# Prompt attention: queries and keys in high and low parts, near scores as three fp32r products of 128 rows, and the third pair's load issued sooner

## The reference, cut to what matters

```python
GROUPS = ((128, 1), (512, 4), (2048, 16))        # (window, dilation)
scale = HEAD_DIM ** -0.5
# for each group, on strided sub-sequences in blocks of 128 queries:
s = jnp.einsum('brnqhc,brnkhc->brnhqk', qg, kb) * scale
s = jnp.where(mask[None], s, NEG_INF)
m = jnp.max(s, axis=-1, keepdims=True)
p = jnp.exp(s - m)
den = jnp.sum(p, axis=-1)
o = jnp.einsum('brnhqk,brnkhc->brnqhc', p, vb) / den[..., None]
# the three groups are combined per head, weighted by den * exp(m - m_top)
```

## Time and profile before

| | us |
|---|---|
| median of 3 runs | 1893.93 (1889.38 to 1894.47) |
| the profiled execution | 1889.74 |
| its span, first to last instruction | 1888.0 |
| mean granted TensorE clock | 0.999 of full |

### The profile page before, as it was taken

One profiled execution on the slowest core, in us unless ns is written; L12 is line 12 of the kernel. 1 busy time (PEld: TensorE's weight loads), 2 busy tenths in 40 slices (PEclk: granted clock), 3 DMA queues, 4 the chain that ended last, 5 costly groups with the idle time before them and its releaser, 6 DMA issues.

```text
span 1888.0 us, 35926 instructions
## 1 busy us (share of the span) xinstructions
PE 1859.1 (98%) x15206; PEld 1772.4 (94%) x15206; DVE 1209.6 (64%) x1507; ACT 710.3 (38%) x948; POOL 666.3 (35%) x339
## 2 busy tenths in 40 slices
PE   8999999999999999999999999999999999999998
PEld 8999999989889898679999999899999999999998
DVE  8899653255444645674456746884555575878988
ACT  6311221244434445664200034424444445433333
POOL 0122111211111113443466641136777761432514
PEclk9999999999999999999999999999999999999999
DMA  5422433766676644642353332533334466655334
GB/s 179 115 90 80 139 114 113 254 195 207 220 223 211 233 155 131 202 122 103 126 203 127 133 122 81 178 123 114 137 136 161 159 209 249 204 196 190 119 136 142
DMA packets 191415, 298.73 MB, mean 158 GB/s; under 512 B 37248, under 2 KB 133248, under 8 KB 187680
## 3 DMA queue, kind: packets, MB, share of 16 engines
q1 hardware_dynamic: 183776, 270.06, 43.9%
q10 hardware_dynamic: 7488, 26.50, 3.5%
HBM read 215.12 MB, written 79.28 MB: 156 GB/s over the span
## 4 chain that ended last, share of the span: by engine, by line
PE 84%; DVE 7%; DMA 3%; issue 2%; POOL 2%; ACT 1%; SPq 1%; POOLq 0%; DVEq 0%; ACTq 0%
PE ps L2674 38%; PE ps L3213 26%; PE ps L3057 3%; PE ps L3013 2%; PE ps L3147 2%; PE ps L2934 1%; PE ps L2847 1%; PE ps L3133 1%; PE ps L2689 1%; PE ps L2828 1%; PE ps L2943 1%; PE ps L2904 1%; PE ps L2809 1%; PE ps L2836 1%; DVE n_tmp L1866 1%
## 5 line engine op out<-in xcount | busy, mean ns | idle before, releaser
L1181 POOL TENSOR_TENSOR w_lo<-w_raw,w_hi 128x1024 fp32r<-128x1024 f32 x48 | 123.0, 2563 | 616.4 <-ACT w_hi L1330 616.4
L2674 PE MATMUL ps<-op_hi,w_hi 128*128 128x352 f32 x1392 | 309.3, 330 | 0.1
L2674 PE MATMUL ps<-op_hi,w_lo 128*128 128x352 f32 x1392 | 300.1, 323 | 0.0
L2674 PE MATMUL ps<-op_lo,w_hi 128*128 128x352 f32 x1392 | 299.3, 323 | 0.0
L2674 PEld LDWEIGHTS ps<-op_hi,w_hi 128*128 128x128 f32 x1392 | 232.8, 189 | 15.3 <-issue 13.2
L2674 PEld LDWEIGHTS ps<-op_hi,w_lo 128*128 128x128 f32 x1392 | 238.3, 188 | 0.0
L2674 PEld LDWEIGHTS ps<-op_lo,w_hi 128*128 128x128 f32 x1392 | 236.5, 188 | 0.0
L1404 ACT ACTIVATE stage<-ps 128x1056 f32<-128x1056 f32 x48 | 50.5, 1052 | 279.3 <-PE ps L2674 279.3
L1188 POOL TENSOR_TENSOR w_hi<-w_raw,zeros 128x1024 fp32r<-128x1024 f32 x24 | 60.3, 2514 | 167.8 <-PE ps L3147 63.0
L3213 PE MATMUL ps<-do_hi,w_hi 128*128 128x264 f32 x560 | 113.9, 285 | 2.3 <-DVE w_lo L2495 1.0
L3213 PE MATMUL ps<-do_lo,w_hi 128*128 128x264 f32 x560 | 113.8, 285 | 0.0
(11 more groups left out here) (483 smaller groups left out, 4614.0 us busy)
## 6 DMA issues: line engine op xcount, KB each, us to landing
w_raw<-in_w SPq DMA_DIRECT2D x101, 512.0 KB, 3.9
t_raw<-tmp_h SPq DMA_DIRECT2D x28, 1056.0 KB, 5.6
kc<-in_k_cache SPq DMA_DIRECT2D x48, 448.0 KB, 5.4
vc<-in_v_cache SPq DMA_DIRECT2D x48, 448.0 KB, 5.8
out_keep<-stage ACTq DMA_DIRECT2D x24, 528.0 KB, 2.7
tmp_gate_d<-stage ACTq DMA_DIRECT2D x24, 528.0 KB, 5.6
gate_t<-tmp_gate_d SPq DMA_DIRECT2D x24, 528.0 KB, 3.5
tmp_h<-o_t SPq DMA_DIRECT2D x18, 528.0 KB, 2.9
```

The lines of the kernel that those rows point to most:

```text
L1181: pool.tensor_tensor(lo, w_raw[:, b], hi.bitcast(F32), ALU.subtract).then_inc(w_split[b], 1)
L2674: mm = pe.matmul(ps[:, 3 * dst + q, 0:BLK], w[:, b, w0 + n], x[:, k, q * BLK:(q + 1) * BLK], start=(n == 0 and part == 0), stop=(n == len( ...
```

## The change

Queries and keys of a pair get a high part each (ScalarE copies them into fp32r tiles; the queries are put into the order of residues on the way) and a low part each (VectorE subtracts). The near scores become three products per head, hi·hi, hi·lo and lo·hi, of 64 rows and all 128 queries of the tile as outputs. The far scores stay as they are. ScalarE makes the next pair's high parts in the first step of a pair (`HIGH_STEP`), VectorE the low parts in the third (`LOW_STEP`), GpSimd the far keys in the second instead of the fifth (`FAR_STEP`). The first pair's parts are made in `bias_make`. TensorE waits for both low parts of a pair (`at_lo`) before its scores. The third pair's load is issued ahead of the loop over pairs, before the second pair's far values. The new tiles lie in space that is free in this stage.

```diff
+HIGH_STEP, FAR_STEP, LOW_STEP = 0, 1, 2
...
             far_values(0)
+            at_load(2)
             for w in range(HP):
                 if w + 1 < HP:
                     far_values(w + 1)
-                if w + 2 < HP:
+                if 0 < w < HP - 2:
                     at_load(w + 2)
...
-                if g % PER == PER - 3 and w < HP:
+                if g % PER == FAR_STEP and w < HP:
...
+            def high_parts(w):
+                act.wait_ge(at_in[w % 2], 48 * (w // 2 + 1))
+                if w >= 2:
+                    act.wait_ge(at_s, PER * (w - 1))
+                elif w:
+                    act.wait_ge(sa_o, ROUNDS)
+                else:
+                    act.wait_ge(lru_h, T_XA)
+                s.activation(hi_of(w)[:, 1], pair_of(w)[:, 1], ACT.Copy).then_inc(at_hi.sem, 1)
+                s.activation(in_blocks(hi_of(w)[:, 0]), queries_by_residue(w), ACT.Copy).then_inc(at_hi.sem, 1)
...
                 at_copy(g)
+                if g % PER == HIGH_STEP and g // PER + 1 < HP:
+                    high_parts(g // PER + 1)
...
+            def low_parts(w):
+                dve.wait_ge(at_far_k, w + 1)
+                if w >= 2:
+                    dve.wait_ge(at_s, PER * (w - 1))
+                past(dve, at_hi, 2 * w + 1)
+                v.tensor_tensor(low_keys_of(w)[:], pair_of(w)[:, 1], hi_of(w)[:, 1].bitcast(F32), ALU.subtract).then_inc(at_lo.sem, 1)
+                past(dve, at_hi, 2 * w + 2)
+                v.tensor_tensor(in_blocks(low_queries[w % 2][:]), queries_by_residue(w), in_blocks(hi_of(w)[:, 0].bitcast(F32)),
+                                ALU.subtract).then_inc(at_lo.sem, 1)
...
+                if g % PER == LOW_STEP and g // PER + 1 < HP:
+                    low_parts(g // PER + 1)
...
                 te.wait_ge(at_far_k, w + 1)
+                past(te, at_lo, 2 * w + 2)
+                q_hi, k_hi, q_lo, k_lo = hi_of(w)[:, 0], hi_of(w)[:, 1], low_queries[w % 2], low_keys_of(w)
...
-                    for x in range(RES):
-                        out = slice(RQ * x, RQ * x + RQ)
+                    for part, (qs, ks) in enumerate(((q_hi, k_hi), (q_hi, k_lo), (q_lo, k_hi))):
                         for a, rows in enumerate(heads):
-                            mm = pe.matmul(ps[out, 2 * (g % 2) + a, first:first + near_keys(q)], queries[a][:, x],
-                                           pair_of(w)[rows, 1, keys:keys + near_keys(q)], start=True, stop=True)
+                            mm = pe.matmul(ps[:, 2 * (g % 2) + a, first:first + near_keys(q)],
+                                           qs[rows, P * q:P * q + P],
+                                           ks[rows, keys:keys + near_keys(q)], start=(part == 0), stop=(part == 2))
```

More of the change, by code:

```diff
@@ L533, in hybrid_layer, with hi_of, in_blocks, queries_by_residue @@
         yo = at("B", 6 * ROW, "yo", [P, 2, T])
+        hi_first = at("BR", 75776, "hi_first", [P, 2, T], F32R)
+        hi_later = [at("B", AREA // 2, "hi_even", [P, 2, T], F32R), at("B", AREA // 2 + 8192, "hi_odd", [P, 2, T], F32R)]
+        low_keys = [at("BR", 4 * T, "low_keys_first", [P, T], F32R)] + [at("A", 4 * T * (3 * n + 1), f"low_keys{n}", [P, T], F32R) for n in range(2)]
+        low_queries = [at("BR", 12288, "low_queries0", [P, T], F32R), at("B", AREA // 2 + 5 * ROW, "low_queries1", [P, T], F32R)]
         v_d = nc.dram_tensor("tmp_v", ((KD - 2) * P, P), F32, kind="Internal").ap()
+        def hi_of(w):
+            return hi_later[w % 2] if w else hi_first
+        def in_blocks(x):
+            return x.rearrange("p (q r i) -> p q r i", q=KD, r=RES)
+        def queries_by_residue(w):
+            return pair_of(w)[:, 0].rearrange("p (q i r) -> p q r i", q=KD, r=RES)
+        def low_keys_of(w):
+            return low_keys[w % 2 + 1] if w else low_keys[0]
         def keys_by_residue(w):
@@ L663, in hybrid_layer @@
         mix_spread = Resumed(lru_xc, T_XA)
+        at_hi, at_lo = Resumed(s5_kpad, S5_N), Resumed(s5_v_read, S5_N)
         JOB = len(UPS)
@@ L812, in at_load @@
             def at_load(w):
-                if w >= 2:
+                if w >= 3:
                     sy.wait_ge(at_s, PER * (w - 1))
@@ L1468, in sample_acts @@
                                  ACT.Copy).then_inc(sa_pt, 1)
+            def high_parts(w):
[8 more added lines that the diff above has]
+                s.activation(in_blocks(hi_of(w)[:, 0]), queries_by_residue(w), ACT.Copy).then_inc(at_hi.sem, 1)
             def act_step(name, n):
+                if name == "bias_make":
+                    high_parts(0)
                 if name in ("turn", "taps", "out"):
@@ L2145, in sample_work @@
                             step(v.tensor_copy(bias_q[q][rows, 2 * P:], bias[rows, c:c + RES * far_keys(q):RES]))
+                    low_parts(0)
             dve.wait_ge(s5_out, S5_N)
```

## The result

| | kernel before | kernel after |
|---|---|---|
| median of the runs | 1893.93 us (1889.38 to 1894.96, 5 runs) | 1928.24 us (1926.09 to 1931.34, 5 runs) |
| ratio, 95% interval | 1 | 1.0191 [1.0178, 1.0204] |
| profiled execution, span | 1889.74, 1888.0 | 1928.24, 1926.5 |

The changed kernel is slower by 1.9%. The direction and the range of the prediction held; its time, 1915, was 13 us short, and what happened lies closest to the rival it called a slow clock (1929). Nearly all of it lies in the attention stage: from TensorE's first near product to its last value product the stage takes 124.6 us before (736.30 to 860.90) and 162.6 after (737.04 to 899.69).

What follows compares the result with a forecast made beforehand. TensorE, without slack in the attention stage, was taken to bound the kernel. 2.5 + 5 + 17.5 - 1.7 = 23.3 us on 1889.74 gave 1913; half the median's 4.2 excess made it 1915 us, range 1898 to 1940.

Steps and rivals of the forecast that it cites:

- a slow clock: Rival, chance 0.14: after each of five new 3.5 us gaps TensorE runs at 1.2 GHz; 14 us on top, 1929.
- VectorE, low parts: At five handovers, TensorE's next scores wait 3.5 us for VectorE's two subtractions: +17.5 us, from 14.5 to 24.
- ScalarE, high parts: At five handovers, ScalarE's two copies delay TensorE's value transposes, 0.8 us each, 1.8 at the first pair: +5 us.
- TensorE, products: Near products in the attention stage: +0.09 us per tile with far keys, -0.13 in the last step; +2.5 us.
- third pair's load: TensorE's 1.66 us wait for this load goes, since it is issued 7 us sooner: -1.7 us, 0 at worst.
- What bounds: Attention stage: TensorE is busy for all of each 19.70 us period, so each microsecond it waits lengthens the end.
- The upper bound of the term (10): ScalarE's handover copies: + 10 us if the strided query copy takes 2.09 us instead of 1.05.
- At nothing: First pair's parts fit idle VectorE and ScalarE time; GpSimd's earlier far keys are the same work: no cost.
- Range: Whole run: 1898 to 1940 us, from the terms' low ends up to both slow rivals.
- Heads in turn: Rival, chance 0.13: fp32r products of 64 rows do not pair on TensorE; its term is 19 instead of 2.5, 1932.
- Not slower: Rival, chance 0.10: TensorE reaches the next scores 2.9 us later anyway, hiding VectorE's low parts; say 1888 us.
- The period: One pair of heads in the attention stage: near 24.4 us (19.70 + 0.4 + 0.8 + 3.5); wrong if below 21.

Runs made afterwards that it cites:

- parts made once: Against the changed kernel: high and low parts made for the first two pairs only, all products kept; 1901.63 us, ratio 1.0049.
- zeros in the wait: Against the changed kernel: TensorE multiplies zeros (13 fp32r products) at each of the five handovers before waiting for the low parts; 1920.88 us, ratio 1.0155.
- the kernel with the load alone: Against the kernel before: only the third pair's load moved ahead of the loop, no parts made; 1891.98 us, ratio 0.9996.
- the kernel with two products: Against the kernel making parts for the first two pairs only: third near product (low queries by high keys) left out; 1896.61 us, ratio 1.0035.
- a lead of three steps: Against the changed kernel: scores three steps ahead instead of four; 1906.86 us, or 1896.08 us with the making of the parts also spread over steps.
- queries in plain order: Against the changed kernel: high and low query parts made in the queries' own order, not by residues; 1918.23 us, ratio 1.0147.

## Why the prediction was right, and where not

By its terms, against the 38.5 us between the spans:

| term | forecast | measured | from |
|---|---|---|---|
| VectorE, low parts | +17.5 | +17.7 | waits after |
| ScalarE, high parts | +5 | +8.4 | waits after |
| TensorE, products | +2.5 | +4.6 | 6 x 0.77, parts made once |
| low clock | 0 (a rival: +14) | +9.6 | 5 x 1.9, zeros in the wait |
| third pair's load | -1.7 | -1.7 | wait gone; alone 1.2 of it comes back |

These give 38.6, closer to 38.5 than the terms are known: the clock's is 9.6 by the periods and 7 by whole runs.

**What bounds.** Right: with no slack in TensorE, each wait came through whole in the stage, which is 38.0 us longer.

**VectorE.** Right in place and in releaser; right in size (3.54 against 3.5) by luck, for two errors cancelled. I added 0.5 for GpSimd's blocking and took both subtractions at 1.21. In fact the strided one takes 1.96, and GpSimd slows neither. I had the order wrong: the first subtraction starts 0.18 us ahead of GpSimd's normalization (809.82 and 810.00), so it is GpSimd that waits. I had charged the wrong engine. The Trainium skill ("SBUF — State Buffer", Who interferes with whom) says just that the later one blocks; 0.99 turning to 3.63 agrees with it.

**ScalarE.** The step that failed is "Only the reading is strided here, so I take 1.05 for it too": reading alone doubles it, to 2.10. That makes the wait 1.38 instead of 0.8 and, at the first pair, 2.88 instead of 1.8. The upper bound of the term (10) had it.

**Products.** The heads pair and entering costs 0.19, both as taken. Two sizes were off: a tile with far keys is 0.13 dearer, not 0.09; and the last step went from 0.84 to 0.88 us instead of down to 0.71. TensorE's timeline of the kernel after shows where: the last step's products of 128 columns start 0.11 to 0.12 us apart, hardly less than those of 256 columns, and I had taken half of 0.118.

```profile
807.33 0.28 PE L2958 MATMUL ps<-low_keys,hi_even 64*128 64x128 f32 x2
807.44 0.28 PE L2958 MATMUL ps<-hi_even,low_queries 64*128 64x128 f32 x2
807.56 0.33 PE L2958 MATMUL ps<-hi_even 64*128 64x256 f32 x2
```

What keeps them apart no run asked.

**Clock.** The largest error of size. The mechanism stood among the rivals, with its gaps and its price (14 for 9.6), but at a chance of 0.14. I had read rows 2 and 11 as evidence against it, though a gap of 1.66 us says nothing of one of 3.5. With the 9.6 and the two sizes above, the sum would have been 1930. That the rival's 1929 lies so near is luck: its price was 4 too high, and the forecast that it was added to was 5.5 too low in ScalarE's and the products' terms. The prediction cited the Trainium skill ("TensorE: Matmul & The Clock Gate", HAM oscillation) with its warning of idle gaps; the trace after agrees (0.50 behind each gap of 3.54 us), and that warning should have moved the chance.

**Load.** "At no cost; if late, TensorE waits in the far products" was in the text as the exception, but for the far values behind the load. Alone, the load delays those of the first pair, which stand in front of it, and 1.18 of the 1.66 us come back. In the changed kernel no wait for the far values appears: their first use is at 765.62, 7.4 us later than in the kernel with the load alone.

**At nothing.** Right as far as the traces go: no wait of TensorE in the stage after names the far keys. The first near products start at 737.04 against 736.30 before, and in the other kernels that make the parts at 735.8 to 737.3, so the first pair's parts cost less than this spreads.

**Range.** Its lower end was added up with 2 for ScalarE, where that term's own lower bound was 0. Nothing hangs on it, since the result lies far above.

**Rivals.** Heads in turn is refuted by the kernel with two products (0.95 us per period less, where heads in turn would give 1.8). "Not slower" is refuted as stated. But its mechanism, TensorE coming later to the first new scores, is what a lead of three steps brings about, and then it is nearly true: 1896. None of the versions beats the kernel before: even with the waits taken away the products still cost 0.77 us per pair.

**The period**: 24.4 forecast; 25.42 with the clock held up; 26.9 and 27.7 with it down.

## What to carry over

Free time of an engine on average does not hide new work: ask how long before its use the work can begin and what already stands between, since here the same instructions cost 4 or 34 us in whole runs, and 9 or 38 in the stage, by that alone. When a change makes TensorE idle for longer than any idle time in the trace, give the low clock behind it a price and a fair chance; shorter gaps without it are no evidence against it. Price a strided read by a strided row, even if only one side is strided.

## What was not expected of the hardware

- Reading every fourth fp32 element of a row of 1024 costs ScalarE's copy twice the time (1.05 to 2.10 us) and VectorE's subtraction from two SBUF tiles 1.6 times (1.22 to 1.96), with the results written side by side. The Trainium skill ("SBUF — State Buffer", Door 1) speaks of a penalty for each access that crosses to a new 16-byte line, which these reads do; the runs agree (2.10 against 1.05 us).
- GpSimd's first normalization ends only behind the second of two subtractions in a row: the two normalizations take 3.63 us where 0.99 is their own time, and 2.94 where the subtractions take 2.4. Between the two subtractions it doesn't get through.
- The granted clock fell at each of the ten gaps of 3.54 and 2.80 us (kernel after, queries in plain order), and at none of the 1.38 us. The length of the gap alone doesn't settle it: the single gap of 2.88 us in the kernel after left the clock at 1.00, and one of 2.86 at the same place, in the kernel that makes the low parts for two pairs, was followed by 3.4 us at 0.50. At the stage's start it is as irregular: in some of the kernels it fell once there too, behind a gap of 1.2 us, in others not.
